# Row blocks of the front in four pieces, step weights in two passes, memory keys turned in one piece, weights' low part behind the turned block

## The reference

```python
def _mem_kv(mem, mem_norm_w, w_mem_kv):            # 256 memory rows -> keys and values, 4 heads x 128
    return (_rmsnorm(mem, mem_norm_w) @ w_mem_kv).reshape(b, m, 2, MEM_HEADS, MEM_HEAD_DIM)

h = _rmsnorm(x, norm_in_w)                         # x: 1024 + 32 rows of 1024
u = h @ w_in
z_ssd, xbc, dt_raw, qkv, z_att, q_mem, z_mem, gate_raw = _split_in(u)
y_ssd = _ssd_branch(z_ssd, xbc, dt_raw, ...)       # dt_raw: 16 columns, softplus -> step sizes
y_att = dilated attention of three head groups (windows 128, 512, 2048; dilations 1, 4, 16) * silu(z_att)
y_mem = _mem_attn(q_mem, mem_kv) * silu(z_mem)
merged = gates[0] * (y_ssd @ w_br_ssd) + gates[1] * (y_att @ w_br_att) + gates[2] * (y_mem @ w_br_mem)
y = _rmsnorm(x + merged @ w_out, norm_f_w)
```

## Time and profile before

| | |
|---|---|
| median of 3 runs | 2289.96 us (2281.03 to 2293.83) |
| profiled execution | 2287.94 us, its span 2286.1 us |
| mean granted TensorE clock | 0.949 |
| PE busy | 2078.8 us (91%), 14586 matmuls |
| PE weight loads busy | 1950.0 us (85%) |
| DVE busy | 994.0 us (43%) |
| ACT busy | 759.6 us (33%) |
| POOL busy | 238.2 us (10%) |
| DMA | 248.75 MB, mean 109 GB/s |
| chain that ended last | PE 76%, DVE 9%, ACT 6%, DMA 5%, issue 4% |

### The profile page before, as it was taken

The page is one execution under the profiler, slowest core; times in us unless marked ns, Lnnn a source line. Parts: engine busy times, 40 slices in busy tenths (PEclk is TensorE's granted clock), DMA queues, the critical chain, the costliest instruction groups (busy, mean ns, idle before and its releaser), DMA issues.

```text
span 2286.1 us, 35321 instructions
## 1 busy us (share of the span) xinstructions
PE 2078.8 (91%) x14586; PEld 1950.0 (85%) x14586; DVE 994.0 (43%) x1952; ACT 759.6 (33%) x1641; POOL 238.2 (10%) x358
## 2 busy tenths in 40 slices
PE   4899998999789999999997879998999978979997
PEld 4799998999789898999997659745999978979897
DVE  5213665525444435353254780200444465544523
ACT  5223343222433323324543111201454554123302
POOL 1000121100001010112222000000111111100000
PEclk9899999999889999999998887999999989999999
DMA  6211242211101111112154673365434264544422
GB/s 214 70 39 57 77 111 65 83 34 49 36 30 62 50 53 57 61 62 89 65 200 146 193 230 105 119 218 161 129 102 135 79 202 129 196 162 167 135 80 101
DMA packets 166848, 248.75 MB, mean 109 GB/s; under 512 B 19653, under 2 KB 114565, under 8 KB 166661
## 3 DMA queue, kind: packets, MB, share of 16 engines
q1 hardware_dynamic: 144432, 179.50, 25.2%
q0 software_dynamic: 22256, 66.98, 8.9%
HBM read 179.73 MB, written 66.70 MB: 108 GB/s over the span
## 4 chain that ended last, share of the span: by engine, by line
PE 76%; DVE 9%; ACT 6%; DMA 5%; issue 4%; SPq 0%; DVEq 0%; POOL 0%; ACTq 0%; POOLq 0%
PE bank L2160 19%; PE bank L2161 18%; PE bank L2162 18%; PE bank L2330 2%; DVE w_lo L1628 2%; PE bank L2305 2%; PE bank L2288 2%; DMA kvring<-in_cache_win_kv 2%; PE bank L2440 1%; PE bank L2555 1%; ACT soft L1441 1%; ACT w_hi L1314 1%; DVE softT L1870 1%; PE bank L2266 1%; DMA w_raw<-in_w_in 1%
## 5 line engine op out<-in xcount | busy, mean ns | idle before, releaser
L2160 PE MATMUL bank<-w_hi,hT_hi 128*128 128x256 f32 (+1 forms) x1872 | 544.6, 291 | 27.4 <-ACT hT_hi L1424 18.8
L2161 PE MATMUL bank<-w_lo,hT_hi 128*128 128x256 f32 (+1 forms) x1872 | 532.2, 284 | 0.0
L2162 PE MATMUL bank<-w_hi,hT_lo 128*128 128x256 f32 (+1 forms) x1872 | 531.2, 284 | 0.0
L2160 PE MATMUL bank<-hT_hi,w_hi 128*128 128x352 f32 x1344 | 459.1, 342 | 16.4 <-DVE w_lo L1628 9.9
L2162 PE MATMUL bank<-hT_hi,w_lo 128*128 128x352 f32 x1344 | 444.1, 330 | 0.0
L2161 PE MATMUL bank<-hT_lo,w_hi 128*128 128x352 f32 x1344 | 444.0, 330 | 0.0
L2160 PEld LDWEIGHTS bank<-w_hi,hT_hi 128*128 128x128 f32 (+1 forms) x1872 | 355.1, 190 | 29.9 <-issue 28.6
L2162 PEld LDWEIGHTS bank<-w_hi,hT_lo 128*128 128x128 f32 (+1 forms) x1872 | 355.8, 190 | 0.8
L2161 PEld LDWEIGHTS bank<-w_lo,hT_hi 128*128 128x128 f32 (+1 forms) x1872 | 355.0, 190 | 0.7
L2160 PEld LDWEIGHTS bank<-hT_hi,w_hi 128*128 128x128 f32 x1344 | 263.1, 196 | 28.4 <-DVE w_lo L1628 10.2
L2161 PEld LDWEIGHTS bank<-hT_lo,w_hi 128*128 128x128 f32 x1344 | 263.6, 196 | 0.5
(11 more groups left out here) (399 smaller groups left out, 2967.5 us busy)
## 6 DMA issues: line engine op xcount, KB each, us to landing
w_raw<-in_w_in SPq DMA_DIRECT2D x96, 512.0 KB, 5.0
kvring<-in_cache_win_kv SPq DMA_DIRECT2D x144, 256.0 KB, 3.6
feat_T<-fstage POOLq DMA_DIRECT2D x40, 528.0 KB, 4.1
fstage<-feat_T SPq DMA_DIRECT2D x16, 528.0 KB, 4.4
kvring<-in_cache_mem_kv SPq DMA_DIRECT2D x32, 256.0 KB, 3.4
xc<-feat_T SPq DMA_DIRECT2D x8, 1024.0 KB, 5.8
o_rows<-obuf POOLq DMA_DIRECT2D x48, 132.0 KB, 2.0
mo<-o_rows SPq DMA_DIRECT2D x24, 264.0 KB, 3.8
```

The source lines that it names most:

```text
L2160: pe.matmul(out, xh(k), wh(k), start=(k == 0), stop=False)
L2161: pe.matmul(out, xh(k), wl(k), start=False, stop=False)
L2162: ins = pe.matmul(out, xl(k), wh(k), start=False, stop=(k == nk - 1))
```

## The change

- A row block is handled in four pieces instead of two, in the order V (`norm_v`: variance, reciprocal, root) of block i, H (`norm_h`: high part) of block i - 1, A (`norm_a`: load and sum of squares) of block i + 1, L (`norm_l`: low part) of block i - 2, X (`norm_x`: scaling and transposes) of block i.
- The eviction of a memory chunk's step becomes a step of its own, `mem_out` (E), later in the list than its T. The load of the first two chunks is a step of its own, `load0`, so that it may stand ahead of the cast.
- `dt` multiplies a 128 x 32 stationary part (high and low weights side by side) with the high and with the low part of the rows: 48 matmuls instead of 72. Its result has 32 rows, which `dt_rows` adds in pairs with nine matmuls against a table `twice` instead of nine transposes. T(v1,0) and T(v1,1) stand ahead of `dt`; its evictions (`dt_out`) behind the casts of chunks 4 and 5.
- A key chunk is turned in one step, four transposes and one copy of 512 columns.
- A `low` step ahead of which the list would go on with a turn is put behind that turn.

```diff
+    twice = eq(i % SH, SH)
...
-                steps = [steps[0], steps[1], ("turn", n, 0), ("turn", n, 1)]
+                steps = [steps[0], steps[1], ("turn", n, 0)]
...
-    sched += [A(0), A(1), B(0), A(2), B(1), ("split0", 0), A(3), B(2), A(4), B(3), T(k0, 0), ("split0", 1), A(5), B(4), T(k0, 1)]
-    sched += [A(6), B(5), turn(k0, 0), turn(k0, 1), T(k1, 0), A(7), B(6), T(k1, 1), ("split", k0), A(8), B(7)]
-    sched += [turn(k1, 0), turn(k1, 1), A(9), B(8), T(v0, 0), ("split", k1), A(10), B(9), ("dt_w",), T(v0, 1), B(10)]
-    sched += [("dt",), T(v1, 0), ("split", v0), T(v1, 1), ("split", v1)]
+    def row_step(i):
+        return [("norm_v", i)] + [("norm_h", i - 1)] * (i >= 1) + [("norm_a", i + 1)] * (i < 10) + [("norm_l", i - 2)] * (i >= 2) + [("norm_x", i)]
+    T, E, turn = (lambda n, t: ("tok", n, t)), (lambda n, t: ("mem_out", n, t)), (lambda n: ("turn", n, 0))
+    between = {2: [("load0", 0)], 3: [("split0", 0), T(k0, 0)], 4: [("load0", 1), T(k0, 1), E(k0, 0)], 5: [E(k0, 1), ("split0", 1), T(k1, 0)],
+               6: [T(k1, 1), turn(k0), E(k1, 0)], 7: [E(k1, 1), ("split", k0), T(v0, 0)], 8: [turn(k1), T(v0, 1), E(v0, 0)],
+               9: [E(v0, 1), ("split", k1), ("dt_w",), T(v1, 0)],
+               10: [("norm_h", 10), ("norm_l", 9), ("norm_l", 10), T(v1, 1), E(v1, 0), ("split", v0)]}
+    sched += [("norm_a", 0)]
+    for i in range(11):
+        sched += row_step(i) + between.get(i, [])
+    sched += [("dt",), E(v1, 1), ("split", v1), ("dt_out",)]
...
-        sched.insert((later[0] if later else i) + 1, ("low", s[1]))
+        at = (later[0] if later else i) + 1
+        sched.insert(at + (sched[at][0] == "turn" if at < len(sched) else 0), ("low", s[1]))
...
-        wdt_hi = sb(stage, "wdt_hi", [P, KT8, SH], F32R)
-        wdt_lo = sb(stage, "wdt_lo", [P, KT8, SH], F32R)
+        wdt = sb(stage, "wdt", [P, KT8, 2, SH], F32R)
...
-            dve.wait_ge(s_const, 32)
             for s in sched:
-                if s[0] == "norm_a":
+                if s[0] == "norm_v":
...
+                elif s[0] == "norm_x":
+                    i = s[1]
+                    m = P if i < 10 else NS
+                    r = small[0:m, i:i + 1]
+                    if i == 0:
+                        dve.wait_ge(s_const, 32)
                     dve.wait_ge(s_rstd, i + 1)
                     x = xin[0:m, i % 3, :]
                     dve.scalar_tensor_tensor(x, x, r, normw[0:m, 0 if i < 2 else 1, :], ALU.mult, ALU.mult).then_inc(s_xn, 1)
-                elif s[0] == "norm_b":
+                elif s[0] == "norm_l":
...
                     if kind == "mk":
-                        dst = KmT[:, 2 * detail:2 * detail + 2, P * t:P * t + P]
+                        src = bank[7][:, :].rearrange("p (t i n) -> p i t n", t=2, i=2)
+                        dst = KmT[:, 2 * detail:2 * detail + 2, :].rearrange("p i (t n) -> p i t n", t=2)
...
                     for j in range(3):
                         cols = slice(THIRD * j, THIRD * j + THIRD)
-                        ins = three(bank[(3, 5, 6)[j]][0:SH, 0:THIRD],
-                                    lambda k: wdt_hi[:, k, :], lambda k: wdt_lo[:, k, :],
-                                    lambda k: hTh[:, k, cols], lambda k: hTl[:, k, cols], KT8)
+                        for k in range(KT8):
+                            pe.matmul(bank[(3, 5, 6)[j]][0:2 * SH, 0:THIRD], wdt[:, k, :, :], hTh[:, k, cols], start=(k == 0), stop=False)
+                            ins = pe.matmul(bank[(3, 5, 6)[j]][0:2 * SH, 0:THIRD], wdt[:, k, :, :], hTl[:, k, cols], start=False, stop=(k == KT8 - 1))
                     ins.then_inc(s_dtp, 1)
...
-                        ins = pe.transpose(bank[3][0:m, SH * t:SH * t + SH], dt_cols[:, P * t:P * t + m], ident[0:SH, 0:SH])
+                        ins = pe.matmul(bank[3][0:m, SH * t:SH * t + SH], dt_cols[:, P * t:P * t + m], table("twice")[0:2 * SH, :], start=True, stop=True)
...
-                    for i in range(2):
-                        ins = pe.transpose(bank[7 if kind == "mk" else 3][:, P * i:P * i + P], rows[:, c % 4, P * i:P * i + P], ident)
+                    for i in range(4 if kind == "mk" else 2):
+                        at = (c + i // 2) % 4
+                        ins = pe.transpose(bank[7 if kind == "mk" else 3][:, P * i:P * i + P], rows[:, at, P * (i % 2):P * (i % 2) + P], ident)
```

More of the change, by code:

```diff
@@ L353, in build_program @@
     turn_of_slot = {slot_of[("tok", s[1], s[2])]: v for s, v in turned.items()}
+    turn_of_slot.update({slot_of[("tok", s[1], 1)]: v for s, v in turned.items() if chunks[s[1]][0] == "mk"})
     roped = {}
@@ L717, in build_program @@
             norms_before[s], turns_before[s], scored_before[s] = nn, nt, ns
-            nn += s[0] == "norm_b"
+            nn += s[0] == "norm_x"
             nt += s[0] == "turn"
@@ L862, in keys_evicted @@
                 eng.wait_ge(s_skD, v + 1 - sum(on_act[:v + 1]))
-        dt_cols = fraw_a[0:SH, 3:3 + TOK]
+        dt_cols = fraw_a[0:2 * SH, 3:3 + TOK]
         def fraw_of(c):
@@ L991, in _ @@
                         sp.dma_start(con[:, P:], io["const"][:, P:]).then_inc(s_par, 16)
-                elif s[0] in ("split0", "split"):
-                    n = s[1] if s[0] == "split0" else s[1] + 2
+                elif s[0] in ("load0", "split"):
+                    n = s[1] if s[0] == "load0" else s[1] + 2
                     if n >= n_chunks:
@@ L1323, in _ @@
                     act.activation(xsq[0:m, :], xin[0:m, i % 3, :], ACT.Square, accum_out=small[0:m, i:i + 1]).then_inc(s_sq, 1)
+                elif s[0] == "norm_v":
+                    i = s[1]
+                    m = P if i < 10 else NS
                     act.wait_ge(s_var, i + 1)
                     act.activation(small[0:m, i:i + 1], small[0:m, i:i + 1], ACT.Sqrt).then_inc(s_rstd, 1)
-                elif s[0] == "norm_b":
+                elif s[0] == "norm_h":
                     i = s[1]
@@ L1338, in _ @@
                     act.wait_ge(s_par, 32)
-                    act.activation(wdt_hi[:, :, :], wdt_raw[:, :, :], ACT.Copy).then_inc(s_dte, 1)
-                elif s[0] == "dt":
+                    act.activation(wdt[:, :, 0, :], wdt_raw[:, :, :], ACT.Copy).then_inc(s_dte, 1)
+                elif s[0] == "dt_out":
                     act.wait_ge(s_dtp, 3)
                     for j in range(3):
-                        ins = act.activation(dt_cols[:, THIRD * j:THIRD * j + THIRD], bank[(3, 5, 6)[j]][0:SH, 0:THIRD], ACT.Copy)
+                        ins = act.activation(dt_cols[:, THIRD * j:THIRD * j + THIRD], bank[(3, 5, 6)[j]][0:2 * SH, 0:THIRD], ACT.Copy)
                     ins.then_inc(s_dte, 1)
@@ L1349, in _ @@
                     act.activation(dtv[0:NS, P:], bank[3][0:NS, P:P + SH], ACT.Copy).then_inc(s_dte, 1)
-                elif s[0] == "tok":
+                elif s[0] == "mem_out" or s[0] == "tok" and chunks[s[1]][0] not in ("mk", "mv"):
                     _, n, t = s
+                    s = ("tok", n, t)
                     kind, detail = chunks[n][0], chunks[n][1]
@@ L1697, in _ @@
                     kind, detail = chunks[n][0], chunks[n][1]
-                    src = bank[7 if kind == "mk" else 3][:, 0:CW].rearrange("p (i n) -> p i n", i=2)
                     if kind == "mk":
-                        dst = KmT[:, 2 * detail:2 * detail + 2, P * t:P * t + P]
+                        src = bank[7][:, :].rearrange("p (t i n) -> p i t n", t=2, i=2)
+                        dst = KmT[:, 2 * detail:2 * detail + 2, :].rearrange("p i (t n) -> p i t n", t=2)
                     else:
+                        src = bank[3][:, 0:CW].rearrange("p (i n) -> p i n", i=2)
                         g, half = detail
@@ L2179, in _ @@
             for s in sched:
-                if s[0] == "norm_b":
+                if s[0] == "norm_x":
                     i = s[1]
@@ L2192, in _ @@
                     pe.wait_ge(s_cv, 16 * 9)
-                    pe.wait_ge(s_turned, 4)
+                    pe.wait_ge(s_turned, 2)
                     pe.transpose(bank[7][:, 0:80], obuf[0:80, 0, 0:P], ident[0:80, 0:80]).then_inc(s_dtp, 1)
@@ L2257, in _ @@
                     if kind == "mk":
-                        pe.wait_ge(s_pjev, proj[("tok", n, t)] + 1)
+                        pe.wait_ge(s_pjev, proj[("tok", n, 1)] + 1)
                     else:
@@ L2284, in _ @@
                         _, g, b, half = u
-                        pe.wait_ge(s_turned, max(turns_before[s], 4 + (2 * g + half + 1) * 2 * NB))
+                        pe.wait_ge(s_turned, max(turns_before[s], 2 + (2 * g + half + 1) * 2 * NB))
                         for h in range(4):
```

6 lines of the change are left out of this document (2 added, 4 removed).

## The result

| | kernel before | changed kernel |
|---|---|---|
| median | 2292.85 us (2281.03 to 2301.77) | 2273.74 us (2272.15 to 2277.1) |
| ratio to before | | 0.993, 95% interval 0.9908 to 0.9952 |
| the same again, beside later experiments | 2293.35 us | 2274.81 us, ratio 0.9924 (0.9906 to 0.9943) |
| profiled execution, span | 2287.94 us, 2286.1 us | 2273.57 us, 2271.8 us |

A forecast was written before the change was run, and what follows sets the result against it. TensorE, with 76% of the chain, was taken as the bound, though not in the front. Front with dt 9.5 us plus low parts 10.7 us gave 20.2 us less, so 2268 us, range 2252 to 2281.

The forecast's parts named there:

- What bounds it: Whole kernel: TensorE has 76% of the chain; only fewer instructions or less standing still or slow running there wins time.
- Part 1, dt: Step weights: 48 matmuls at 0.160 us instead of 72, 5.8 us less, 3.8 sure and 2.0 depending on the clock.
- The price of dt_rows: In dt_rows, nine ordinary matmuls take 1.1 us where nine transposes took 0.70: +0.4 us, bounds 0 and 1.9.
- The upper bound of 1.9: In dt_rows: 1.9 us if each of the nine matmuls takes the 0.292 us of a slow dt matmul.
- Part 2, the front: Front in four pieces: features start at 86.3 instead of 94.64; 9.5 us won including dt, bounds 3.5 and 14.
- rival (b): Front gives only dt's 3.8 us, its new order eats the rest: 2274 to 2280 us; chance 0.18.
- Part 3: Eleven low parts behind the turn's copy: 6.2 us of waits and 4.5 of clock, 10.7 us; bounds 5 and 22.
- its list of signs: Behind the moved low parts: scores don't wait, the turn waits up to 1 us for the mask in the wide form.
- The sum: Whole kernel: 9.5 + 10.7 = 20.2 us less, said as 2268 us; chance 0.55.
- Rival (c): Attention stage's moved low parts bring 5 us only, the front its 9.5: 2273 us; chance 0.10.
- One sign of being wrong: Whole kernel: the forecast is wrong if the clock falls at other places instead.
- Rival (d): Front: a block's load behind a weight load on SP comes late, 10 us per period: slower, 2298; chance 0.05.

The follow-up runs named there:

- e1: Kernel before with only the eleven low parts put behind the turn copy that follows them: 2278.5 us, ratio 0.9943 to before.
- e6: Changed kernel with transposes in the row step, ten low parts behind the mask and the first key chunk's load covered: 2258.18 us, ratio 0.9857 to before.
- e8: Changed kernel with a third pass of 24 matmuls, its sum overwritten, ahead of dt's two: 2275.13 us in one execution.
- e10_before_covered: Kernel before with the first key chunk's cast and low part two row blocks later: 2289.59 us, ratio 0.9992 to before.
- e2: Changed kernel with the low parts back at their old place, so dt and front alone: 2290.11 us, ratio 1.0005 to before.
- e4: Changed kernel with ten low parts one turn copy later, past the mask: 2271.17 us, ratio 0.9909 to before.
- e5: Changed kernel with the first key chunk's cast and low part two row blocks later: 2268.65 us, ratio 0.9894 to before.
- e9: Changed kernel with low parts at their old place and the first key chunk's cast and low part two row blocks later: 2283.96 us, ratio 0.9962 to before.
- e3: Changed kernel with nine transposes for dt_rows' nine matmuls, halves added on VectorE: 2269.88 us, ratio 0.9914 to before.

## Why the prediction was right, and where it was not

**What bounds it** held: no gain came from busy time, all from TensorE standing still or slow for less long.

**Part 1, dt.** The 48 matmuls ran at 0.160 us and the clock was up, as forecast; the third pass shows that each 24 cost 3.83 us there. The price of dt_rows failed: 0.4 us was forecast, 2.9 us were measured, 1.4 in the step and the rest in the clock behind it. The step that failed is a count. I read the value products of the earlier trace rows as sixteen in 1.89 us, 0.12 each. Those sixteen are records: the unit has four heads and two key blocks, so eight matmuls, each of which the trace shows as two records, 0.236 us each. The nine of dt_rows stand as 18 records in the same way. Nine times 0.236 is 2.1 us, which is what they took (2.04); the row had the right price, read per instruction. The upper bound of 1.9 held for the step and not with its clock. The rule in the Trainium skill's page Perfetto Trace Analysis, section Transposes, spoke for the larger price; the trace agrees with it (2.04 us as matmuls, 0.64 as transposes, start to start), and I had set it aside for a row that I had miscounted.

**Part 2, the front.** The simulation was close: T(k0,0) forecast at 27.0 and found at 25.99, the first turn's copy 48.0 and 48.02, the start of the features 86.3 and 87.05. Of the forecast 9.9 us 9.2 came (94.64 + 1.6 - 87.05); less 2.9 for dt_rows this is 6.3, the lead up to 390 us. What was missing is the step after the sum: I took a lead won at 87 us to last until the end. 4.4 of the 6.3 us went at 412 to 452. The queue that this would have needed was there to read: a 1.17 us wait behind a weight load, with evictions and rope queued behind cast and low part. The size was not: neither the load's further 1.8 us nor the 2.6 us of low clock stand in the trace of before. For the front, rival (b), worth only dt's share, comes nearest, for a reason that it did not name.

**Part 3.** The mechanism was right: the wait changes its owner, to the turn behind the mask's first half. Sizes: net waits 8.5 us for 6.2, clock about 4.0 for 4.5, the lead 12.5 us with the part alone for 10.7. What a place gives was taken too low: each of the four wide ones gave 0.82 us for 0.60 (at the one that was 552.62 in the kernel before, a wait of 1.04 us became 0.22), and of the six narrow ones four gave 0.67 for 0.3 (1.92 at 770.00 became 1.25) and two 0.24. The three windows stand at 1.00 as forecast. The turn's wait is 1.1 us at two wide places and 0.2 at the other two, where "up to 1 us" was said, and up to 1.26 in the narrow form, of which its list of signs says nothing.

**The sum.** Forecast 9.5 + 10.7 = 20.2. In the trace 6.3 - 4.4 + 13.3 gives 15.2, the 15.5 of mark 34 but for 0.3; the medians differ by 19.1 and 18.5 us. A term too high by 3.2, one missing at -4.4, and one too low by 2.6 leave the sum 5.0 us too high against this trace, a quarter of it. That the medians come within 2 us of 20.2 is in part luck, of the kind that makes two executions of the changed kernel differ by 1.5 us at mark 34 and 6.5 at mark 63. The 2268 us said was 5.7 us off, 2.9 of them because the later median of the kernel before is that much slower than the one that the prediction started from. Rival (c) named 2273, nearest to the measured 2273.74, and its mechanism is refuted on both counts: part 3 brought 12.5 us alone and not 5, the front alone nothing and not 9.5. One sign of being wrong did appear: the clock fell at other places, behind dt_rows (101 us) and behind the stop at 426.75. Rival (d), a block's load too late behind a weight load, has no row: between 14 and 87 us ScalarE waits for no load at all.

**What stays open.** Why the load takes 7.4 us instead of 5.6. Over the twelve traces it took 5.3 to 5.9 us in four (before, e1, e6, e8) and 6.9 to 7.9 in the other eight. Most of the kernels with the rebuilt front are slow there, but the front doesn't settle it: e10_before_covered, whose order up to this load is that of the kernel before, took 7.29 us, and e6_all_three, which has the front, 5.39. A transfer on the queue for instructions lies between issue and landing in seven of the eight slow ones. From the changed kernel, 414.32 to 421.73:

```profile
q1 hardware_dynamic: 1056, 1.05, 45.8%
q0 software_dynamic: 98, 0.09, 8.5%
q8 instruction: 1, 0.02, 0.8%
```

The eighth, e10 (421.98 to 429.29), has none:

```profile
q1 hardware_dynamic: 1056, 1.05, 46.7%
q0 software_dynamic: 100, 0.10, 8.7%
```

And e6, fast, has one, though only 0.6 us before its landing. So that transfer is not needed for a slow load, and no run moved it by itself. Open too is what decides whether the clock falls behind one and the same stop.

## What to carry to other kernels

A lead won early can be spent at a later wait for a load that has nothing between it and TensorE: follow the marks of both traces through to the end, and at each place where a cast or split waits for a load, see what is queued behind it that does not need it. When two engines hand work around in fixed order, moving an item one place moves the wait to the next item behind it; move it into idle time instead, here past the mask. Before a row's time is divided by its count, hold the count against the instructions in the code; and where a rule contradicts the row so read, widen the term to the rule's end.

## What the runs showed of the hardware

- A plain fp32 matmul appears as two records and takes 0.23 us with 16 columns (nine as 18 records in 2.04 us) as with 64 (eight as 16 in 1.89), where a transpose is one record and takes 0.08.
- The nine matmuls were followed by a fall of the granted clock to about 0.5, for some 3.4 us, in all seven traces that have them (the changed kernel twice, e2, e4, e5, e8, e9), and by none in the two with transposes there (e3, e6).
- The same stop of 2.95 us in the same place of the same program is followed by a clock of 0.58 in one execution and 1.00 in another, which is worth 2.6 us; a stop of 1.91 us at 525 us left it at 1.00 in the kernel before and brought 0.66 in e2, and 0.71 in e10, which has the kernel before's order there.
- Two executions of one program, within 0.03 us at mark 16, differ by 6.5 us at mark 63, as much as most parts of this change are worth: a term of a few us can be read from marks near its place, and not from one time of the whole.
